# Where a norm and its first panel stand in a decoder step: the program's head as one stage by thirds of the tokens, and the second mixer's norm inside the first MLP's last part

## The chip, the cores and the metric

The kernel runs on one core of one Trainium2 chip. The metric is the device time of one execution in microseconds (us); lower is better. A core has five engines that run their own instruction streams and meet through semaphores: TensorE (PE in the profile, with its weight loads as PEld), VectorE (DVE), ScalarE (ACT), GpSimd (POOL) and SyncE (SP), which here only issues DMAs.

## The reference

One step of a decoder with two layers over 1,056 tokens: 1,024 of a prompt and 8 sequences of 4 sample tokens. Width 1,024, float32 throughout.

```
for l in range(DEPTH):                     # DEPTH = 2
    if l < N_SELF:                         # layer 0: mLSTM matrix memory ("first mixer")
        mix, (c, n, m) = mlstm_layer(rmsnorm(h, norm_mix[l]), ..., w_in_a[l], ..., w_out_a[l])
    else:                                  # layer 1: stick-breaking attention ("second mixer")
        kv = rmsnorm(h, norm_kv) @ w_kv
        q = (rmsnorm(h, norm_mix[l]) @ w_q_b[j])
        o = stick_breaking_attention(q, k_all, v_all, sb_bias[j], past_len)
        mix = o @ w_out_b[j]
    h = h + mix
    u = rmsnorm(h, norm_mlp[l]) @ w_up[l]
    h = h + jnp.square(jax.nn.relu(u)) @ w_down[l]
y = rmsnorm(h, norm_final)
```

`rmsnorm(x, g)` is `x * rsqrt(mean(x*x) + 1e-6) * g`, over the features of a token.

## The kernel before

**Layout.** The residual `h` stays in SBUF with features on partitions: `m.h` is [128, 8, 1056], 8 feature tiles (`KT`) of 128. Tokens are cut into three thirds (`NT = 3`) of 352 (`TW`). Each float32 product is made of three matmuls: x is split into `x_hi` (rounded) and `x_lo` (the rest), each weight panel of 128 output features into `w_hi` and `w_lo`, and hi*hi, lo*hi and hi*lo are added in PSUM. One output tile (128 features by a third of the tokens) is 24 matmuls of 128x352, a panel is three tiles, 72 matmuls.

**Weights.** There are two weight slots. SP loads a panel into `w_raw[slot]`, POOL splits it (`split_panel`: a multiply by the norm's gain where there is one, a CAST to `w_hi`, a TENSOR_TENSOR to `w_lo`), and PE uses it. The first two panels of a mixer or MLP are loaded and split at the end of the part before (`head_loads`, `head_splits`; class `Head` holds their semaphores).

**Norm.** `rms` is not applied before the product: panels are multiplied with the raw split of h, and `rms_inverse` scales the result when it is read from PSUM. So a norm is: on ACT `x_hi` (8 ACTIVATEs) and squares (8), on DVE `x_lo` (8) and the sum of the squares (`norm_add`, 8), on PE one matmul per third with a matrix of ones (`norm_pe`), on ACT a Ln per third and one Exp (`norm_act_rs`). `dense_first` runs the first panel feature tile by feature tile while `x_lo` is being made: the 9 matmuls of tile k wait for x count k+1.

**Order.** The program is a chain of phases, each an `nc.Block`: all engines finish one before any begins the next.

1. `constants`: POOL fills masks and the identity; SP loads five gains and the page table.
2. `embed`: SP loads nine row blocks of x, PE transposes them (4 transposes to a bank, 4 banks), DVE and ACT copy the banks to `h` by turns; POOL splits the first two panels.
3. `mixer_a`: on ACT and DVE the norm of all tokens, on PE the gate panel (`w_in_a`'s last 128 columns), then the norm's sums; POOL meanwhile makes fills (`filled`, 12 of them) and then splits. DVE scales the gate rows into `graw`, PE picks the 16 gate rows out (L830), and DVE runs a long chain over 8 rows from L1052 on, while PE runs the first four panels. Each panel tile goes to one of two banks and waits for the bank's read-out by DVE, which stands inside that chain. ACT spills `h` to HBM (`h_spill`), for the residual.
4. `out_and_mlp`: output projection, then 8 chunks of 4 up panels and 4 down double-panels. Down tiles are added to `h` by DVE. The chunks are a hardware loop.
5. `mixer_b`: semaphores are cleared and the engines meet once more, then SP loads the biases, two panels, spills `h`, and loads pages of the cache; ACT, DVE and PE do the norm and the first panel (q). Then come the k panel (3 tiles), page transposes, the v panel, and the attention.
6. `out_and_mlp` again, and `final`.

Of the kernel before, what the change touches and what calls it, by code (L numbers as in the profile page):

```python
# [106 lines left out]
def weight_turns(eng, stages, panel):  # L107

    n = tiles = before = 0
    for turns, panels in stages:  # L110
        per, per_tiles = len(panels), sum(x[1] for x in panels)
        assert per % 2 == 0
# [65 lines left out]
class Head:  # L178
# [3 lines left out]
    def __init__(self, own, panels):  # L182
        self.w, self.panels = weight_sems(own.sem), panels


def head_loads(sp, m, head, w=None, panels=0):

    for slot, (ap, _) in enumerate(head.panels):
        if w is not None:

            sp.wait_ge(w.split, panels - 1 + slot)
        load_panel(sp, m, head.w, slot, ap)
# [36 lines left out]
def dense_first(pe, m, w, n, slot, before, x, between=None):  # L229
# [6 lines left out]
    for k in range(KT):  # L236
        if k == KT // 2 and between is not None:
            between()
        pe.wait_ge(x, k + 1)
        for t in range(NT):  # L240
            wh, wl = m.whi[slot][:, k * P:(k + 1) * P], m.wlo[slot][:, k * P:(k + 1) * P]
            xh, xl = m.xhi[:, k, t * TW:(t + 1) * TW], m.xlo[:, k, t * TW:(t + 1) * TW]
            pe.matmul(m.bank[t][:, 0:TW], wh, xh, start=(k == 0), stop=False)
            pe.matmul(m.bank[t][:, 0:TW], wh, xl, start=False, stop=False)
            last = pe.matmul(m.bank[t][:, 0:TW], wl, xh, start=False, stop=(k == KT - 1))
            if k == KT - 1:
                last.then_inc(w.tile_ready, 1)
# [57 lines left out]
def norm_pe(pe, m, s):  # L305

    pe.wait_ge(s.acc, KT)
    for t in range(NT):
        pe.matmul(m.bank[3 + t][:, 0:TW], m.ones[:, :], m.acc[:, t * TW:(t + 1) * TW], start=True, stop=True)\
# [3 lines left out]
def norm_act_rs(act, m, s):  # L313

    for t in range(NT):
        act.wait_ge(s.sum, t + 1)
        act.activation(m.rs[:, t * TW:(t + 1) * TW], m.bank[3 + t][:, 0:TW], ACT.Ln, bias=m.eps[:, 0:1],
# [6 lines left out]
def constants(nc, m, own):  # L324

    made, landed = own.sem("constants_made"), own.sem("gains_landed")
    with nc.Block() as block:
        @block.gpsimd
        def _(pool):
            pool.memset(m.ident[:, :], 0.0).then_inc(made, 1)  # L330
            pool.memset(m.identb[:, :], 0.0).then_inc(made, 1)
            pool.memset(m.ones[:, :], 1.0).then_inc(made, 1)
# [5 lines left out]
            pool.memset(m.eps[:, :], EPS).then_inc(made, 1)  # L338
            pool.wait_ge(made, 9)
            n = 9  # L340
# [8 lines left out]
            keep(m.ident[:, :], ALU.not_equal, 1.0, 0, [[-1, P]], 1)  # L349
# [8 lines left out]

            for j in range(SG):
# [4 lines left out]

        @block.sync
        def _(sp):
            gains = [(m.g_mix[l], m.d["norm_mix"][l]) for l in range(2)]
            gains += [(m.g_mlp[l], m.d["norm_mlp"][l]) for l in range(2)]
            gains += [(m.g_kv, m.d["norm_kv"])]
            with nc.allow_non_contiguous_dma(reason="five gains of 4 KB, a feature to a partition"):  # L370
                for tile, src in gains:
                    sp.dma_start(tile[:, :], src.rearrange("(k p) -> p k", p=P)).then_inc(landed, 16)
            sp.dma_start(m.ptab[:, :], m.d["page_table"].rearrange("b (o g) -> o (b g)", o=1)).then_inc(landed, 16)
            sp.wait_ge(landed, 16 * len(gains) + 16)

def embed(nc, m, own):

    with ExitStack() as c:  # L380
        xin = own.tensor("x_rows", [P, NB, D], F32)
        landed = [own.sem(f"x_landed{b}") for b in range(NB)]
        turned, free_dve, free_act = own.sem("x_turned"), own.sem("x_bank_free_dve"), own.sem("x_bank_free_act")
        block = c.enter_context(nc.Block())

        @block.sync
        def _(sp):
            for b in range(NB):
                t0, n = blocks_of(b)
                src = m.d["x_prompt"][0, t0:t0 + n, :] if b < NC else m.d["x_sample"].rearrange("b t d -> (b t) d")  # L390
                sp.dma_start(xin[0:n, b, :], src).then_inc(landed[b], 16)
            head_loads(sp, m, m.heads[0])

        @block.gpsimd
        def _(pool):
            head_splits(pool, m, m.heads[0])

        @block.tensor
        def _(pe):
            g = 0  # L400
            for b in range(NB):
                n = blocks_of(b)[1]
                pe.wait_ge(landed[b], 16)
                for half in range(2):
                    if g >= 4:

                        pe.wait_ge(free_act if g % 2 else free_dve, (g - 4) // 2 + 1)
                    for q in range(4):
                        k = 4 * half + q
                        last = pe.transpose(m.bank[g % 4][:, q * P:q * P + n], xin[0:n, b, k * P:(k + 1) * P],  # L410
                                            m.ident[0:n, 0:n])
                    last.then_inc(turned, 1)
                    g += 1

        def read_out(eng, op, which, free):
            for g in range(which, 2 * NB, 2):
                t0, n = blocks_of(g // 2)
                eng.wait_ge(turned, g + 1)
                src = m.bank[g % 4][:, :].rearrange("p (q t) -> p q t", q=4)[:, :, 0:n]
                op(m.h[:, 4 * (g % 2):4 * (g % 2) + 4, t0:t0 + n], src).then_inc(free, 1)  # L420

        @block.vector
        def _(dve):
            read_out(dve, dve.tensor_copy, 0, free_dve)

        @block.scalar
        def _(act):
            read_out(act, act.copy, 1, free_act)
# [87 lines left out]
def mixer_a(nc, m, own):  # L516
# [66 lines left out]
    with ExitStack() as c:  # L583
# [25 lines left out]
        w, s = m.heads[0].w, norm_sems(own.sem)  # L609
        filled, landed = own.sem("fills"), own.sem("a_landed")  # L610
        spilled, gathered = own.sem("h_spilled"), own.sem("pages_gathered")
# [20 lines left out]
        panels = [(lambda i: last128, NT), (lambda i: last128, 0)] + [panel_in(*x) for x in PANELS]  # L632
# [34 lines left out]
        def _(pool):  # L667
# [22 lines left out]
            head_splits(pool, m, m.heads[1], w, (TILES - NT, TILES))  # L690

        @block.tensor
        def _(pe):
            def third(tau, part):

                n = (tau - TAU0) // NT + 2
                t = tau % NT
                bank = m.bank[tau % 2]
                if part == 0:
                    pe.wait_ge(w.split, n + 1)  # L700

                    pe.wait_ge(w.tile_free[0], tau - 1)
# [129 lines left out]
            for tau in range(TAU0, TAU0 + FIRST_TILES):  # L832
# [33 lines left out]
        def _(act):  # L866
            norm_act(act, m, s, m.h, m.g_mix[0])
            for kk in range(KT):
                act.dma_start(m.spill[kk], m.h[:, kk, :]).then_inc(spilled, 16)
            norm_act_rs(act, m, s)  # L870
# [140 lines left out]
        def _(dve):  # L1011
            norm_dve(dve, m, s, m.h, m.g_mix[0])
# [29 lines left out]
            for t in range(NT):  # L1042
# [3 lines left out]
                dve.tensor_tensor(graw[:, ts], m.bank[t][:, 0:TW], m.rs[:, ts], ALU.mult).then_inc(w.tile_free[0], 1)  # L1046
# [172 lines left out]
def mixer_b(nc, m, own):  # L1219
# [61 lines left out]
    with ExitStack() as c:  # L1281
# [17 lines left out]
        w, s = m.heads[2].w, norm_sems(own.sem)  # L1299
        landed, spilled, filled, chain = own.sem("b_landed"), own.sem("h_spilled"), own.sem("fills"), own.sem("dve_step")  # L1300
# [60 lines left out]
        def _(eng):  # L1361
# [15 lines left out]
            for kk in range(KT):  # L1377
# [729 lines left out]
```

## Time and profile before

| | |
|---|---|
| median of 3 runs | 3087.38 us (3086.38 to 3090.63) |
| profiled execution | 3094.23 us |
| its span, first to last instruction | 3092.4 us |
| PE busy | 2893.2 us, 94% |
| DVE / ACT / POOL busy | 45% / 26% / 24% |
| granted TensorE clock, mean | 0.974 |

A row of the timeline gives start and duration of a group of like instructions on one engine, its line, what it writes and reads, and in brackets how long the engine stood idle before it and what ended the wait. The times below are of the profiled execution and count from its first instruction.

### The profile page before, as it was taken

The numbers are of one execution on the slowest core, as the hardware profiler recorded it, in microseconds if no ns is written. First come the engines' busy times: TensorE is split into PE (matmuls) and PEld (weight loads), VectorE is DVE, ScalarE is ACT, GpSimd is POOL, SyncE is SP. The second block draws the span as 40 slices with busy tenths as digits, with TensorE's granted clock in tenths as the row PEclk, the third lists the DMA queues.
The fourth block names the chain that finished last, engine by engine and source line by source line (L and its number), as shares of the span: only waits on it lengthen the run. The fifth ranks groups of instructions, "written<-read, shape, count | busy, mean of one in ns | idle before, by whom it ended". The sixth has DMA issues, their size and how long they took to land. (4 is left out here: it accounts for less than half of the span.)

```text
span 3092.4 us, 49344 instructions
## 1 busy us (share of the span) xinstructions
PE 2893.2 (94%) x19749; PEld 2634.2 (85%) x19749; DVE 1378.7 (45%) x1993; ACT 818.4 (26%) x1647; POOL 756.2 (24%) x452
## 2 busy tenths in 40 slices
PE   5999997999999999978999899898799999999998
PEld 4989887999999999976766677666599999999997
DVE  4422334444433344444546554655545433344434
ACT  3120222211110011124555545555512110011112
POOL 4212111322323323332111211120122332332331
PEclk8999998999999999989999999999899999999999
DMA  5666444233233232223333433343411111111112
GB/s 160 177 149 193 83 29 92 73 92 96 81 95 95 81 95 87 89 97 96 107 109 98 121 97 114 100 119 91 147 48 42 48 42 47 47 41 47 47 41 77
DMA packets 362482, 277.68 MB, mean 90 GB/s; under 512 B 31394, under 2 KB 353954, under 8 KB 360290
## 3 DMA queue, kind: packets, MB, share of 16 engines
q1 hardware_dynamic: 341002, 258.18, 28.8%
q10 hardware_dynamic: 21336, 17.47, 2.9%
q8 instruction: 104, 1.70, 0.2%
q14 instruction: 40, 0.33, 0.0%
HBM read 251.58 MB, written 91.11 MB: 111 GB/s over the span
## 5 line engine op out<-in xcount | busy, mean ns | idle before, releaser
L162 POOL CAST w_hi<-w_raw 128x1024 fp32r<-128x1024 f32 x194 | 208.6, 1075 | 1661.1 <-PE bank L214 902.0
L212 PE MATMUL bank<-p_u_hi,w_hi 128*128 128x352 f32 x1536 | 496.5, 323 | 14.5 <-DVE p_u_lo L2001 14.5
L212 PE MATMUL bank<-x_hi,w_hi 128*128 128x352 f32 x1536 | 496.9, 323 | 2.9 <-DVE p_q L1758 2.9
L213 PE MATMUL bank<-p_u_lo,w_hi 128*128 128x352 f32 x1536 | 495.5, 323 | 0.0
L214 PE MATMUL bank<-p_u_hi,w_lo 128*128 128x352 f32 x1536 | 495.3, 322 | 0.0
L214 PE MATMUL bank<-x_hi,w_lo 128*128 128x352 f32 x1536 | 494.5, 322 | 0.0
L213 PE MATMUL bank<-x_lo,w_hi 128*128 128x352 f32 x1536 | 494.0, 322 | 0.0
L164 POOL TENSOR_TENSOR w_lo<-w_raw,w_hi 128x1024 fp32r<-128x1024 f32 x194 | 483.8, 2494 | 15.6
L2009 DVE TENSOR_TENSOR h<-bank,h 128x352 f32<-128x352 f32 x384 | 199.9, 524 | 492.5 <-PE bank L214 492.5
L1961 ACT ACTIVATE p_relu<-bank 128x352 f32<-128x352 f32 x192 | 89.1, 464 | 1039.5 <-PE bank L214 1033.2
L212 PEld LDWEIGHTS bank<-p_u_hi,w_hi 128*128 128x128 f32 x1536 | 288.5, 188 | 18.7 <-issue 18.7
L212 PEld LDWEIGHTS bank<-x_hi,w_hi 128*128 128x128 f32 x1536 | 289.1, 188 | 4.7 <-issue 4.7
L213 PEld LDWEIGHTS bank<-x_lo,w_hi 128*128 128x128 f32 x1536 | 290.0, 189 | 0.0
L214 PEld LDWEIGHTS bank<-x_hi,w_lo 128*128 128x128 f32 x1536 | 289.3, 188 | 0.0
L214 PEld LDWEIGHTS bank<-p_u_hi,w_lo 128*128 128x128 f32 x1536 | 288.6, 188 | 0.0
L213 PEld LDWEIGHTS bank<-p_u_lo,w_hi 128*128 128x128 f32 x1536 | 288.6, 188 | 0.0
L1785 DVE TENSOR_TENSOR_SCAN square<-square,zero 128x512 f32<-128x512 f32 (+5 forms) x192 | 212.7, 1131 | 124.1 <-ACT square L1643 122.3
L1997 DVE TENSOR_TENSOR p_relu<-p_relu,rms_inverse 128x352 f32<-128x352 f32 x192 | 133.4, 695 | 275.5 <-ACT p_relu L1961 275.5
L1999 DVE CAST p_u_hi<-p_relu_sq 128x352 fp32r<-128x352 f32 x192 | 162.9, 849 | 108.5 <-ACT p_relu_sq L1963 108.5
L706 PE MATMUL bank<-x_hi,w_hi 128*128 128x352 f32 x576 | 200.0, 347 | 0.0
L708 PE MATMUL bank<-x_hi,w_lo 128*128 128x352 f32 x576 | 186.2, 323 | 0.0
L707 PE MATMUL bank<-x_lo,w_hi 128*128 128x352 f32 x576 | 185.8, 323 | 0.0
(247 smaller groups left out, 4587.7 us busy)
## 6 DMA issues: line engine op xcount, KB each, us to landing
k_pages<-in_cache_k SPq DMA_DIRECT2D x64, 512.0 KB, 5.7
w_raw<-in_w_up SPq DMA_DIRECT2D x64, 512.0 KB, 4.0
v_pages<-in_cache_v SPq DMA_DIRECT2D x64, 512.0 KB, 4.8
w_raw<-in_w_down SPq DMA_DIRECT2D x64, 512.0 KB, 3.4
p_pages<-k_pages SPq DMA_DIRECT2D x256, 128.0 KB, 2.4
p_pages<-v_pages SPq DMA_DIRECT2D x256, 128.0 KB, 2.3
w_raw<-in_w_in_a SPq DMA_DIRECT2D x26, 512.0 KB, 4.5
h<-h_spill ACTq DMA_DIRECT2D x16, 528.0 KB, 8.6
```

Source lines behind the costliest of these rows:

```text
L162: pool.tensor_copy(m.whi[slot][:, :], m.wraw[slot][:, :]).then_inc(w.hi, 1)
L164: pool.tensor_tensor(m.wlo[slot][:, :], m.wraw[slot][:, :], f32(m.whi[slot][:, :]), ALU.subtract)\
L212: pe.matmul(bank[:, 0:TW], wh, xh, start=(k == 0), stop=False)
L213: pe.matmul(bank[:, 0:TW], wh, xl, start=False, stop=False)
L214: last = pe.matmul(bank[:, 0:TW], wl, xh, start=False, stop=(k == nk - 1))
L706: pe.matmul(bank[:, 0:TW], wh, xh, start=(kk == 0), stop=False)
L707: pe.matmul(bank[:, 0:TW], wh, xl, start=False, stop=False)
L708: last = pe.matmul(bank[:, 0:TW], wl, xh, start=False, stop=(kk == KT - 1))
L1785: dve.tensor_tensor_scan(stick, stick, m.zero[:, 0:1].broadcast_to([P, hi - lo]), sticks[h2][:, hi:hi + 1] if x else 1.0, ALU.mult, ALU.ad ...
L1997: dve.tensor_tensor(relu[t][:, :], relu[t][:, :], m.rs[:, toks], ALU.mult).then_inc(scaled, 1)
L1999: dve.tensor_copy(uhi[:, u, toks], sqr[t][:, :]).then_inc(hi_ready, 1)
L2009: dve.tensor_tensor(ht, m.bank[t][:, 0:TW], ht, ALU.add).then_inc(w.tile_free[t], 1)
```

## The change

**Head.** `constants` and `embed` become one phase, `start`, that also holds the first norm. SP loads x first (three blocks, then the gate panel, then the rest), and the gains last; ACT's queue loads the one gain that the first norm needs. Work goes by thirds of the tokens (row blocks 0 to 2, 3 to 5, 6 to 8): copies to `h`, `x_hi` and `x_lo` of that third, then the gate panel's tile of that third on PE. Squares of a third are one ACTIVATE of 128x2816, and are added pairwise by DVE (1408, 704, 352 columns). PE sums a third at a time. ACT copies two banks of three, DVE one. `h` is spilled from SP's queue. POOL splits the gate panel and, in the other slot, the first real panel. `mixer_a` then starts with that panel's first tile, the fills and `graw`.

**Boundary.** The first `out_and_mlp` gets `norm_after = 1`: its eighth chunk is taken out of the loop. After the three adds of feature tile k, ACT makes `x_hi` and the square of it, DVE `x_lo` and the sum; SP spills it. After the last down tile PE runs the q panel (`dense_first`, now to banks 5 to 7) with the norm's sums ahead of its feature tile 6. `mixer_b` loses all of this and starts with the k panel. The negated biases move behind the fifth read-out.

```diff
-def dense_first(pe, m, w, n, slot, before, x, between=None):
+def dense_first(pe, m, w, n, slot, before, x, between=None, at=KT // 2, bank0=0):
...
+        @block.tensor                       # start()
...
+            for g in range(2 * TO[1]):
+                turn(g)
+            gates(0)
+            for g in range(2 * TO[1], 2 * NB):
+                turn(g)
+            gates(1)
+            pe.wait_ge(made, 2)
+            wait_taken(pe, 2 * NB)
+            sums(0)
+            gates(2)
+            sums(1)
+            sums(2)
...
+        @block.scalar
...
+            copies(0)
+            high(0)
+            copies(1)
+            high(1)
+            square(0)
+            copies(2)
+            high(2)
+            square(1)
+            square(2)
+            act.wait_ge(made, 2)
+            norm_act_rs(act, m, s, 2)
...
-            dense_first(pe, m, w, 0, 0, 0, s.x)     # mixer_a, PE
-            norm_pe(pe, m, s)
+            for part in range(len(THIRDS)):
+                third(TAU0, part)
             pe.wait_ge(w.tile_free[0], NT)
             pe.wait_ge(filled, 12)
-            pe.wait_ge(s.rs, 1)
...
@@ mixer_b, SP
             for n in range(2, 4):
                 weights(n)
-            for kk in range(KT):
-                eng.dma_start(m.spill[kk], m.h[:, kk, :]).then_inc(spilled, 16)
@@ mixer_b, PE, ACT, DVE
-            dense_first(pe, m, w, 0, 0, 0, s.x)
-            norm_pe(pe, m, s)
-            norm_act(act, m, s, m.h, None)
-            norm_act_rs(act, m, s)
-            norm_dve(dve, m, s, m.h, None)
@@ out_and_mlp, SP
+                for k in range(KT):
+                    for t in range(NT):
+                        sp.wait_ge(w.tile_free[t], USES_OUT + (CH - 1) * USES_C + UT + k + 1)
+                    sp.dma_start(m.spill[k], m.h[:, k, :]).then_inc(after.spilled, 16)
@@ out_and_mlp, PE
+            if norm_after:
+                turn(CH - 1, 0)
+                def sums():
+                    pe.wait_ge(w.tile_free[2], USES_OUT + CH * USES_C)
+                    norm_pe(pe, m, after.s, 2)
+                dense_first(pe, m, after.w, 0, 0, 0, after.s.x, between=sums, at=KT - 2, bank0=5)
@@ out_and_mlp, ACT
+                turn(CH - 1)
+                for k in range(KT):
+                    for t in range(NT):
+                        act.wait_ge(w.tile_free[t], USES_OUT + (CH - 1) * USES_C + UT + k + 1)
+                    act.activation(m.xhi[:, k, :], m.h[:, k, :], ACT.Copy).then_inc(after.s.hi, 1)
+                    norm_square(act, m, after.s, m.h, k)
+                norm_act_rs(act, m, after.s, 2)
@@ out_and_mlp, DVE
+                    if ending:
+                        dve.wait_ge(after.s.hi, k + 1)
+                        dve.tensor_tensor(m.xlo[:, k, :], m.h[:, k, :], f32(m.xhi[:, k, :]), ALU.subtract).then_inc(after.s.x, 1)
+                        norm_add(dve, m, after.s, k)
```

Two places show what moves. DVE at the head of the program before, from its first instruction to the start of the gate chain:

```order
L420 COPY h<-bank 128x4x128 x8
L420 COPY h<-bank 128x4x32
L284 SCALAR_TENSOR_TENSOR x_lo<-h,g_mix,x_hi 128x1056 x8
L292 COPY squares<-square 128x1056
L295 TENSOR_TENSOR squares<-squares,square 128x1056 x7
L1046 TENSOR_TENSOR square<-bank,rms_inverse 128x352 x3
L1052 TENSOR_SCALAR p_numerator<-bank,p_gate_bias 8x352
```

and of the change, up to the last `x_lo`; the three adds of lines 515 to 519 then follow twice more:

```order
L462 COPY h<-bank 128x4x128 x2
L509 SCALAR_TENSOR_TENSOR x_lo<-h,g_mix,x_hi 128x352 x8
L462 COPY h<-bank 128x4x128 x2
L509 SCALAR_TENSOR_TENSOR x_lo<-h,g_mix,x_hi 128x352 x8
L462 COPY h<-bank 128x4x128 x2
L515 TENSOR_TENSOR p_x_rows<-p_x_rows 128x1408
L517 TENSOR_TENSOR p_x_rows<-p_x_rows 128x704
L519 TENSOR_TENSOR squares<-p_x_rows 128x352
L509 SCALAR_TENSOR_TENSOR x_lo<-h,g_mix,x_hi 128x352 x8
```

The norm's work is now between the copies, in pieces of a third, and only the last third's stands behind the last copy.

DVE around the boundary of the first MLP and the second mixer before (the last add of the loop, then the mixer):

```order
L2009 TENSOR_TENSOR h<-bank,h 128x352
L284 SCALAR_TENSOR_TENSOR x_lo<-h,x_hi 128x1056 x8
L292 COPY squares<-square 128x1056
L295 TENSOR_TENSOR squares<-squares,square 128x1056 x7
L1747 TENSOR_SCALAR p_minus_bias<-p_bias 128x16
L1748 TENSOR_SCALAR p_minus_bias_sample<-p_bias_sample 128x8
L1758 SCALAR_TENSOR_TENSOR p_q<-bank,rms_inverse 128x352 x3
```

and of the change, feature tiles 0, 1 and 7 of the last chunk and what follows:

```order
L2126 TENSOR_TENSOR h<-bank,h 128x352 x3
L2129 TENSOR_TENSOR x_lo<-h,x_hi 128x1056
L292 COPY squares<-square 128x1056
L2126 TENSOR_TENSOR h<-bank,h 128x352 x3
L2129 TENSOR_TENSOR x_lo<-h,x_hi 128x1056
L295 TENSOR_TENSOR squares<-squares,square 128x1056
...
L2126 TENSOR_TENSOR h<-bank,h 128x352 x3
L2129 TENSOR_TENSOR x_lo<-h,x_hi 128x1056
L295 TENSOR_TENSOR squares<-squares,square 128x1056
L1849 SCALAR_TENSOR_TENSOR p_q<-bank,rms_inverse 128x352 x3
```

Two instructions over 1,056 columns now stand between the adds that free PE's banks; the mixer starts with the read-out of q.

## Rows read from the trace of the kernel before

**Rows 1.** The page: busy time, PE's busy tenths in 40 slices.

```profile
PE 2893.2 (94%) x19749; PEld 2634.2 (85%) x19749; DVE 1378.7 (45%) x1993; ACT 818.4 (26%) x1647; POOL 756.2 (24%) x452
PE   5999997999999999978999899898799999999998
```

**Rows 2.** Timeline of PE, 0 to 70 us.

```profile
14.08 6.24 PE L410 MATMUL bank<-identity,p_x_rows 128*128 128x128 f32 x40 [14.08 <-DMA p_x_rows<-in_x_prompt]
57.99 3.76 PE L309 MATMUL bank<-squares,ones 128*128 128x352 f32 x6 [8.11 <-DVE squares L295]
65.22 3.56 PE L830 MATMUL bank<-square,p_pick_gates 128*128 128x352 f32 x6 [3.47 <-DVE square L1046]
68.35 0.59 PE L706 MATMUL bank<-x_hi,w_hi 128*128 128x352 f32 x1
```

**Rows 3.** Timelines of ACT, DVE, SP and POOL, 2 to 90 us.

```profile
2.27 1.09 SPq L372 DMA_DIRECT2D g_mix<-in_norm_mix  x2
10.27 3.87 SPq L391 DMA_DIRECT2D p_x_rows<-in_x_prompt  x8
16.08 0.58 ACT L420 COPY h<-bank 128x512 f32<-128x512 f32 x1 [14.07 <-PE bank L410]
33.02 0.20 POOL L668 MEMSET p_pick_gates<- 128x128 f32 x1 [0.31 <-POOLq L380]
41.59 2.04 ACT L270 ACTIVATE square<-h 128x1056 f32<-128x1056 f32 x2
40.59 1.58 POOL L686 COPY p_pair_rows<-identity 8x512 f32<-8x512 f32 x1
61.19 1.44 ACT L317 ACTIVATE rms_inverse<-bank,eps 128x352 f32<-128x352 f32 x3 [7.46 <-PE bank L309]
63.77 1.39 DVE L1046 TENSOR_TENSOR square<-bank,rms_inverse 128x352 f32<-128x352 f32 x3 [5.84 <-ACT rms_inverse L320]
68.93 0.57 DVE L1052 TENSOR_SCALAR p_numerator<-bank,p_gate_bias 8x352 f32<-8x352 f32 x1 [3.77 <-PE bank L830]
86.66 0.50 DVE L1038 TENSOR_TENSOR p_v_next<-bank,rms_inverse 128x352 f32<-128x352 f32 x1
```

**Rows 4.** Timeline of PE, 1340 to 1402 us.

```profile
1346.00 0.32 PE L214 MATMUL bank<-p_u_hi,w_lo 128*128 128x352 f32 x1
1383.33 0.63 PE L212 MATMUL bank<-x_hi,w_hi 128*128 128x352 f32 x1 [2.90 <-DVE p_q L1758]
1400.76 1.07 PE L1536 MATMUL bank<-p_page_keys_t,p_q_sample 128*32 128x512 f32 x8 [0.68 <-ACT p_page_keys_t L1684]
```

**Rows 5.** Timelines of DVE, POOL and SP, 1346 to 1383 us.

```profile
1346.50 1.90 POOL L158 TENSOR_TENSOR w_raw<-w_raw,g_kv 128x1024 f32<-128x1024 f32 x1 [5.95 <-issue]
1349.68 2.34 POOL L164 TENSOR_TENSOR w_lo<-w_raw,w_hi 128x1024 fp32r<-128x1024 f32 x1
1353.60 0.32 POOL L1420 MEMSET p_q_sample<- 128x256 f32 x1 [1.59 <-POOLq L2085]
1364.91 11.59 DVE L295 TENSOR_TENSOR squares<-squares,square 128x1056 f32<-128x1056 f32 x7
1370.67 2.70 POOL L158 TENSOR_TENSOR w_raw<-w_raw,g_kv 128x1024 f32<-128x1024 f32 x1 [16.75 <-PE bank L245]
1355.50 0.62 SPq L1372 DMA_DIRECT2D w_raw<-in_w_kv  x1
```

**Rows 6.** Writers of w_raw, 1353 to 1400 us: its last line.

```profile
DMA to landing us min/median/max: 13.3/13.7/14.1
```

**Rows 7.** Windows: busy time of PE, PEld, DVE, ACT, POOL; PEclk, DMA share, GB/s.

```profile
1383.00:1389.00 6.00, 5.67 (x19) 5.70 (x20) 0.97 (x4) 0.00 (x0) 0.00 (x0) 0.50 0.02 5
1353.60:1364.00 10.40, 7.86 (x33) 7.89 (x34) 9.26 (x8) 9.86 (x10) 0.32 (x1) 0.60 0.04 1
```

**Rows 8.** Timeline of PE in the first MLP's own norm.

```profile
604.69 1.94 PE L309 MATMUL bank<-squares,ones 128*128 128x352 f32 x6
606.19 0.59 PE L243 MATMUL bank<-x_hi,w_hi 128*128 128x352 f32 x1
```

More of the change, by code:

```diff
@@ L236, in dense_first @@
     for k in range(KT):
-        if k == KT // 2 and between is not None:
+        if k == at and between is not None:
             between()
@@ L378, in embed @@
[L378 to L396, printed above, removed]
+            split(1)
@@ new lines, in sums @@
+            def sums(t):
+                pe.wait_ge(s.acc, t + 1)
+                pe.matmul(m.bank[2 + t][:, 0:TW], m.ones[:, :], m.acc[:, t * TW:(t + 1) * TW], start=True, stop=True)\
+                    .then_inc(s.sum, 1)
+            for g in range(2 * TO[1]):
[7 more added lines that the diff above has]
+            sums(0)
@@ new lines, in _, with take, copies, high @@
+            gates(2)
+            sums(1)
+            sums(2)
+        def take(eng, op, free, g):
+            t0, n = blocks_of(g // 2)
+            eng.wait_ge(turned, g + 1)
+            src = m.bank[g % 4][:, :].rearrange("p (q t) -> p q t", q=4)[:, :, 0:n]
+            op(m.h[:, 4 * (g % 2):4 * (g % 2) + 4, t0:t0 + n], src).then_inc(free, 1)
+        @block.scalar
+        def _(act):
+            with nc.allow_non_contiguous_dma(reason="a gain of 4 KB, a feature to a partition"):
+                act.dma_start(m.g_mix[0][:, :], m.d["norm_mix"][0].rearrange("(k p) -> p k", p=P)).then_inc(gain_in, 16)
+            def copies(t):
+                for g in range(2 * TO[t - 1] if t else 0, 2 * TO[t]):
+                    if g % AT_DVE:
+                        take(act, act.copy, free_act, g)
+            def high(t):
+                ts = slice(t * TW, (t + 1) * TW)
+                wait_taken(act, 2 * TO[t])
+                if t == 0:
+                    act.wait_ge(gain_in, 16)
+                for k in range(KT):
+                    act.activation(m.xhi[:, k, ts], m.h[:, k, ts], ACT.Copy, scale=m.g_mix[0][:, k:k + 1]).then_inc(s.hi, 1)
+            def square(t):
+                ts = slice(t * TW, (t + 1) * TW)
+                act.activation(squares[t].rearrange("p (k t) -> p k t", k=KT), m.h[:, :, ts], ACT.Square).then_inc(s.sq, 1)
+            copies(0)
[9 more added lines that the diff above has]
+            norm_act_rs(act, m, s, 2)
@@ L422, in _, with copies, low @@
         @block.vector
         def _(dve):
[L424 to L428, printed above, removed]
+            def copies(t):
+                for g in range(2 * TO[t - 1] if t else 0, 2 * TO[t]):
+                    if g % AT_DVE == 0:
+                        take(dve, dve.tensor_copy, free_dve, g)
+            def low(t):
+                ts = slice(t * TW, (t + 1) * TW)
+                for k in range(KT):
+                    dve.wait_ge(s.hi, t * KT + k + 1)
+                    dve.scalar_tensor_tensor(out=m.xlo[:, k, ts], in0=m.h[:, k, ts], scalar=m.g_mix[0][:, k:k + 1],
+                                             in1=f32(m.xhi[:, k, ts]), op0=ALU.mult, op1=ALU.subtract).then_inc(s.x, 1)
@@ L1832, in _, with out_and_mlp @@
                         sample_queries(pq)
-def out_and_mlp(nc, m, own, w_out, w_up, w_down, gain, gather, head, after):
+def out_and_mlp(nc, m, own, w_out, w_up, w_down, gain, gather, head, after, norm_after):
     with ExitStack() as c:
```

229 lines of the change are left out of this document (143 added, 86 removed).

## The prediction

> **What bounds the kernel now.** I read the page first: PE is busy 94% of the span, and its tenths are below 8 in two places that the change touches, the first slice and the eighteenth [rows 1]. So what the change can give is PE's idle and half-speed time there. Then I read PE's timeline in both places, row by row, for what ended each idle stretch. At the head PE waits for the first rows of x until 14.08, for the sum of the squares until 57.99 and for the gate rows until 65.22; DVE starts its chain over the gate rows at 68.93 [rows 2, 3]. At the boundary the last down tile ends at 1346.3, and the k panel, the first that needs the norm to be over, starts at 1383.33 [rows 4]. The reader should see that in both places the chain runs over ACT and DVE: one norm over 1,056 tokens, with PE beside it and then behind it.
>
> **The head, step by step.** What PE does later hangs on the start D of DVE's chain, 68.93 now: read-outs of PE's two banks stand inside it, and PE's first tiles cannot run ahead. The read-out at 86.66 is the sharpest case: PE's sixth tile needs that bank, free at 87.2, and comes to it at 68.35 + 5 x 3.84 = 87.5 now [rows 2]. In the change the first tile is done before the pick, so PE comes one tile (3.84 us, 24 matmuls at 0.16) earlier to that bank and is held there. The tile done early is therefore worth 0.3 us, and the gain is the shift of D.
>
> D after, from the program's start: x is issued where the gains are now, at 2.27 instead of 10.27 [rows 3], so PE has the first rows at 6.1 instead of 14.1. The copies of the first third need about 5 us more: 11. From there ACT is the longest chain. A piece of 352 columns takes it 1.44/3 = 0.48, a square of 1,056 columns 1.02 [rows 3], so 2,816 columns about 2.6. Three times 8 pieces 11.5, three squares 7.8, the copies left 4.5 (8 at 0.58), 1 of waits: 36. DVE then adds the last third's squares: 2,464 columns at the 1.66 us per 1,056 of the adds now (11.59/7) [rows 5] would be 3.9, undisturbed less, I take 3: 39. Sum, Ln and Exp took 57.99 to 63.77 for three thirds [rows 2, 3]; two of the three are done earlier: 3.5. So the mixer's phase starts at S = 43, with ends 42 and 46 (PE at half speed in the two gate tiles that ACT's copies wait for).
>
> What is late next is POOL. The pick needs the 12 fills, and they run from 33.02 to 42.17 [rows 3], 9.2 us, now hidden beside x_lo and the gate panel. In the change their cover is one tile of PE and graw (1.39). They may be shorter without DVE's big operations beside them; no row shows how much. I bound them by 9.2 and by 6.5, which has the copy (1.58 for 8 rows) and the two selects before it at a third, and take 8. The pick and its wait take 68.93 - 65.22 = 3.7 at half speed, about 2 at full speed; after a tile of matmuls I take 3. D = 43 + 8 + 3 = 54, and **the head gives 15 us**; ends: 42 + 6.5 + 2 = 50.5 gives 18, 46 + 9.2 + 3.7 = 58.9 gives 10. The first weight split after the fills is not late: PE has two tiles of the panel before it left, 7.7 us, for 3.4 us of POOL.
>
> **The boundary.** In the last chunk DVE gets two operations per feature tile. Undisturbed, from the last down tile of k: add 0.5, ACT's x_hi 1.1 and its latency 0.3, x_lo 1.25, the sum 1.35, next add 0.5: 5.0 us, and PE needs that bank back after three tiles, 5.8 us. So nothing is late in even k. In odd k POOL splits a panel at the same moment. DVE's seven adds took 11.59; POOL's split began at 1370.67, so about four lie before it, 1.4 each, and three share the 5.8 us behind it, 1.9 to 2.0 each [rows 5]. Then x_lo and sum are 4.0 instead of 2.6, and PE stalls 0.6 to 1 in k = 1, 3 and 5. I take 2.5 in all, with ends 0 and 4. The upper end is a wait for whole operations: x_lo is due 2 us after the tile, POOL's w_lo (2.34) runs from 1.3 to 3.7 behind it, and where the gain's multiply (1.90) comes first, w_lo meets the sum instead [rows 5]; 1.2, 1.2 and 1.8 us make 4.2. The Trainium skill (page "SBUF — State Buffer", section "SBUF: two separate sides") has that as the rule: DVE with two SBUF inputs and GpSimd exclude each other for a whole instruction. By that rule the term is 4.2 instead of 2.5.
>
> Then PE: q panel 72 x 0.16 = 11.5, the sums 606.19 - 604.69 = 1.5 [rows 8] and 0.3 of tail, behind which ACT's Ln and Exp are hidden; end of the phase and cleared semaphores 1.6 (POOL's 1353.60) [rows 5]. The mixer starts at 1346.3 + 2.5 + 11.5 + 1.5 + 0.3 + 1.6 = 1363.7, and PE with the k panel there instead of at 1383.33: 19.6 us.
>
> Not all of it lasts. The v panel starts at 1401.8 now, when the page transposes end [rows 4]. It needs w_raw of v, which SP issues behind the biases: 1.9 us after the mixer's start, and it lands 13.3 to 14.1 later [rows 5, 6], since nothing moves until 1364 (DMA share 0.04, 1 GB/s) [rows 7]. Now the norm hides that. In the change it is 15.2 after the start, POOL's split with gain is 5.5 (1346.50 to 1352.02) [rows 5]: v can start 20.7 after the mixer does. PE alone would be there after 1401.8 - 1383.3 = 18.5, less 3 at full speed, 15.5; so it waits, first for pages, which SP issues behind that panel, and then for the split. v starts at 1363.7 + 20.7 = 1384.4, 17.4 us earlier. After idle of 2.90 us PE ran at clock 0.50 for 6 us [rows 4, 7], which costs half of it; the k panel has that now too, the v panel does not, and after a wait of 3 to 5 us it would: I take 1.5 off. **The boundary gives 16 us**; ends: 11 (all stalls, v panel at half speed for long), 23 (v's panel lands early, full speed: 19.6 and the 3 us that half speed costs now). The spill moves to SP's idle queue in the MLP and costs nothing; uncovered it would be 3.4 us, DVE's wait before the first read-out of q now. Unrolling a chunk and one phase fewer I put at nothing.
>
> **Sum.** 15 + 16 = 31 us: 3094.2 to 3063 in the profiled execution. That one is 6.8 us above the median of the three runs; I take the difference over: 3087.4 - 31 = **3056**. A measurement of this kernel tells about 0.2%, 6 us, from no change.
>
> **The rivals.**
> *The boundary gives everything* (chance 0.12). For it: 8 us of the empty DMA time lie in the biases' small reads, and if v's panel gets in front of them, PE goes through. Against it: the landings of 13.3. Gain 15 + 23 = 38, with a good head 41: 3046 to 3050.
> *The head gives little* (0.16). If PE is at half speed through gate panel and pick, S is 46 or later and DVE's adds are slowed by the split of the second panel. Gain 5 to 10 there, 16 at the boundary: about 3064.
> *The last chunk is paced by DVE and POOL* (0.09): operations wait for each other whole. For it: a 2.3 us operation of POOL meets DVE's in each odd tile; against it: DVE's adds beside POOL went on at 2.0 each [rows 5]. The stalls are 4.2, or up to 8 where even tiles inherit the delay, x_lo and the sum of the last tile come late too, and v's split meets the k read-outs: gain 15 + 8 = 23, 3064. It is the rule of the page named above.
> *No change* (0.03): both PE waits come back in full, the gate chain behind the fills and the k panel behind the pages; needs 31 us of new waits, of which I find 9.
> *Slower* (0.03), one mechanism: in the last chunk each feature tile holds its bank until DVE has done x_lo and sum. Above 5.8 us per tile that delay is PE's. It decides from 31/8 = 3.9 us beyond that, 9.7 per tile; I find 5.0 to 6.9. At 11 us per tile it would be 3087 + 11 = 3098.
>
> **Chances.** Forecast (gain 25 to 37, 3050 to 3062) 0.57, the rivals as given. Faster 0.94, same 0.03, slower 0.03. The range holds the forecast and most of the three gaining rivals: 3046 to 3067.
>
> **What would show it.** Right: DVE's first TENSOR_SCALAR of the gate chain at 54, behind PE's pick, which POOL's copy of pair rows releases; the mixer's phase starting at 43; PE's first matmul of the k panel at about 1363.7 less the head's 15, with an idle of under 2 us before it; and a wait of 3 us or more ahead of the v panel, for POOL's split. Wrong: PE idle over 1 us between down tiles of the last chunk; the fills done before PE's first tile ends; page transposes at once behind the k panel.

## The result, and the profile after

The changed kernel takes 3059.85 us (median of 4 runs, 3056.07 to 3063.72), the kernel before 3088.77 beside it: ratio 0.9907, 95% interval 0.9889 to 0.9925. That is 28.9 us. The two profiled spans are 3061.9 and 3092.4 us, 30.5 apart. The forecast was 3056 with a gain of 31, its range 3046 to 3067.

The page after, with PE's tenths and the granted clock. The first slice has gone from 5 to 7, the eighteenth from 7 to 8 [rows 1].

```profile
span 3061.9 us, 49302 instructions
PE 2885.6 (94%) x19749; PEld 2625.2 (86%) x19749; DVE 1377.0 (45%) x2007; ACT 821.6 (27%) x1661; POOL 751.6 (25%) x450
PE   7999997999999999988898899888799999999998
```

**The head.** Timelines of PE, POOL and DVE of the changed kernel, which answer to [rows 2, 3].

```profile
20.11 1.94 PE L425 MATMUL bank<-identity,p_x_rows 128*128 128x128 f32 x8 [4.54 <-DVE h L462]
46.56 0.63 PE L812 MATMUL bank<-x_hi,w_hi 128*128 128x352 f32 x1 [2.01 <-PEq L328]
52.93 2.01 PE L935 MATMUL bank<-square,p_pick_gates 128*128 128x352 f32 x6 [0.42 <-POOL p_pair_rows L791]
...
46.52 0.20 POOL L773 MEMSET p_pick_gates<- 128x128 f32 x1 [21.39 <-POOLq L328]
51.78 0.19 POOL L785 TENSOR_SCALAR_AFFINE_SELECT p_pick_gates<-p_pick_gates 128x8 f32<-128x8 f32 x1
52.18 0.60 POOL L791 COPY p_pair_rows<-identity 8x512 f32<-8x512 f32 x1
...
13.92 5.44 DVE L509 SCALAR_TENSOR_TENSOR x_lo<-h,g_mix,x_hi 128x352 fp32r<-128x352 f32 x8 [2.42 <-ACT x_hi L480]
55.09 0.57 DVE L1152 TENSOR_SCALAR p_numerator<-bank,p_gate_bias 8x352 f32<-8x352 f32 x1 [7.08 <-PE bank L935]
72.50 0.50 DVE L1138 TENSOR_TENSOR p_v_next<-bank,rms_inverse 128x352 f32<-128x352 f32 x1
```

Read it from the end: DVE's chain over the gate rows starts at 55.09 instead of 68.93, behind PE's pick; the pick waited 0.42 us for POOL's copy of the pair rows, the last of the fills, which run from 46.52 to 52.78. The read-out that stood at 86.66 [rows 3] stands at 72.50: the head gave 14.2 us.

**The boundary.** Timelines of PE, SP, POOL and DVE where the second mixer starts; [rows 4, 5] have the same places before.

```profile
1347.56 0.40 PE L212 MATMUL bank<-x_hi,w_hi 128*128 128x352 f32 x1 [1.66 <-PEq L2210]
1369.18 1.07 PE L1635 MATMUL bank<-p_page_keys_t,p_q_sample 128*32 128x512 f32 x8 [0.68 <-ACT p_page_keys_t L1777]
...
1347.89 1.46 SPq L1467 DMA_DIRECT2D p_bias_sample<-in_sb_bias  x2
1349.40 0.62 SPq L1473 DMA_DIRECT2D w_raw<-in_w_kv  x1
1356.94 13.05 SPq L1490 DMA_DIRECT2D p_pages<-k_pages  x16
...
1362.75 1.89 POOL L158 TENSOR_TENSOR w_raw<-w_raw,g_kv 128x1024 f32<-128x1024 f32 x1 [14.91 <-DMA w_raw<-in_w_kv]
1365.92 2.35 POOL L164 TENSOR_TENSOR w_lo<-w_raw,w_hi 128x1024 fp32r<-128x1024 f32 x1
```

The k panel starts at 1347.56, 35.8 us earlier than in [rows 4]; the products with the page keys, behind which the v panel starts, at 1369.18 instead of 1400.76, 31.6 us earlier. Less the head's 14.2 the boundary gave 21.6 and then 17.4; of the two spans' difference of 30.5 it has 16.3. What held PE between the two stands in the list of PE's waits from 1280 to 1500 us (total, times, longest):

```profile
PE bank L1585 <- DMA p_pages<-k_pages: 5.5, 1, 5.5
PE bank L212 <- DVE h L2126: 1.4, 2, 0.7
```

The wait of 5.5 is for the key pages. POOL's split of v ends at 1368.3 (1365.92 + 2.35), two microseconds before PE starts the v panel (its first matmul stands at 1370.18).

### The profile page after: what moved, and what is told of

It is laid out like the page before. It is cut to its first block and busy times, and to the rows that moved or that the text cites. A ratio compares the mean times of both kernels' runs of the same rounds, so it can differ in the third digit from the quotient of the medians.

```text
span 3061.9 us, 49302 instructions
## 1 busy us (share of the span) xinstructions
PE 2885.6 (94%) x19749; PEld 2625.2 (86%) x19749; DVE 1377.0 (45%) x2007; ACT 821.6 (27%) x1661; POOL 751.6 (25%) x450
## 5 line engine op out<-in xcount | busy, mean ns | idle before, releaser
L164 POOL TENSOR_TENSOR w_lo<-w_raw,w_hi 128x1024 fp32r<-128x1024 f32 x193 | 480.8, 2491 | 15.5
```

What stands on the lines that cost most here:

```text
L164: pool.tensor_tensor(m.wlo[slot][:, :], m.wraw[slot][:, :], f32(m.whi[slot][:, :]), ALU.subtract)\
```

## The experiments

Each is the changed kernel with one edit, unless it says otherwise; "before" is the run of that kernel beside it.

### The halves apart

```diff
 head only:      new start and mixer_a; out_and_mlp and mixer_b as before
 boundary only:  constants, embed, mixer_a as before; out_and_mlp and mixer_b of the change
```

> The new start phase and its first mixer, with the MLP and the second mixer as before. If the two halves of the gain are independent and the head's share is the shift of DVE's gate chain (68.93 before, 55.09 after), this run is 14 us faster than before (13 to 15), and DVE's gate chain starts at 55. If the profiled 14 at the head were partly given back later in the first mixer, it is 10 or less faster; if the head carries more than the profile shows, 18 or more.

> The constants, embed and first mixer as before, with the norm in the MLP's last chunk. If the boundary's share is the rest of what the trace shows (v panel 31.6 us earlier, 14.4 of them from the head), this run is 15 to 17 us faster than before, with 1.4 us of PE stalls in the last chunk and a wait of about 5.5 us for the key pages ahead of the v panel. Rival: the two halves share something (the k_pages gather, the queue), and then the sum of this run and the head-only run misses the 29 us of the change by more than 4.

Head only: 3071.39 us (before 3086.78), ratio 0.9951 [0.9934, 0.9967], 15.4 us. Boundary only: 3071.24, ratio 0.9947 [0.9934, 0.9961], 15.5 us. In the second, PE stalls 1.4 us in the last chunk and waits 5.46 us for the pages. The sum, 30.9, is the change's 28.9 within what such medians tell (the runs of the head alone go from 3064.5 to 3079.6): nothing that the halves share shows.

### The queue behind the boundary: biases and pages

```diff
 mixer_b, SP (biases behind weights)
-    bias, sbias: three small loads      # 8 KB, and twice 2 KB of every second bias
     weights(2); weights(3)              # w_raw of v and q
+    bias, sbias: three small loads
     load_page(0..15)
 biases early: the same three loads stand in out_and_mlp's SP, behind head_loads
 of the last chunk; their two tiles are allocated ahead of the phases' own
```

> The change, with the three bias loads behind the two weight loads and ahead of the pages. Theory A, the biases hold up what is issued behind them: v's weights land about 4 us after issue, POOL's split begins before 1354 instead of 1362.75, but the pages are still behind the biases, so the wait ahead of the page transposes stays at 4 to 7 us and the time is that of the change within 2 us. Theory B, the v panel hangs on POOL's split: the v panel starts 5 us earlier and the kernel is 4 to 5 us faster than the change.

> The change, with the three small bias loads taken out of the second mixer's queue and issued in the MLP's last chunk. Theory A, the biases' small reads hold up the queue: v's weights land about 3 to 5 us after their issue instead of 13.2, POOL's split of v begins before 1353 instead of at 1362.75, PE goes from the k panel to the page transposes without a wait, and the v panel starts at about 1364.7 instead of 1370.25: 5 us faster than the change (4 to 6), 34 faster than before. Theory B, the first reads of the phase are late for another reason (w_raw or the queue itself): v's weights still land 10 us or more after their issue and the time is that of the change within 1 us. Theory C, the pages come in time and the wait moves on to the q panel's split: 1 to 3 us faster.

Behind the weights: 3061.32 us (before 3088.92), ratio 0.992 [0.9905, 0.9936], no gain over the change, as theory A has it (its four runs lie between 3052.1 and 3067.7, so the time alone says little). Timelines of POOL, SP and PE of that run:

```profile
1353.25 1.90 POOL L158 TENSOR_TENSOR w_raw<-w_raw,g_kv 128x1024 f32<-128x1024 f32 x1 [5.59 <-DMA w_raw<-in_w_kv]
...
1352.67 16.50 SPq L1489 DMA_DIRECT2D p_pages<-k_pages  x16
...
1364.06 3.86 PE L1584 MATMUL bank<-identity,p_pages 128*128 128x128 f32 x16 [4.99 <-DMA p_pages<-k_pages]
```

The split of v begins 5.9 us after the phase's start instead of 15.2, and PE still waits 4.99 us for a page: the split was not what the v panel hung on. The list of loads of that run shows what the pages stand behind (KB each, median us to landing):

```profile
w_raw<-in_w_kv SPq DMA_DIRECT2D x1, 512.0 KB, 5.7
p_bias_sample<-in_sb_bias SPq DMA_DIRECT2D x2, 2.0 KB, 9.8
```

and in the change, where they stand first:

```profile
p_bias_sample<-in_sb_bias SPq DMA_DIRECT2D x2, 2.0 KB, 10.0
```

Two kilobytes take longer than 512, in either place. The Trainium skill (page "DMA: Bandwidth & Descriptors", section "Rules for kernel authors") says that a strided last dimension becomes one descriptor for each element; these loads are of that kind (every second bias, 4 bytes), and the count of packets agrees: 1,488 under 512 bytes from 1346 to 1375 us of the change, 340 from 1340 to 1375 in the run below, which has these loads elsewhere. Two loads of 512 elements are 1,024 of the difference. That the number of packets is what makes them slow is not shown.

Early: 3042.78 us (before 3086.78), ratio 0.9857 [0.9841, 0.9873]. POOL, PE and DVE of that run:

```profile
1343.58 0.32 POOL L1514 MEMSET p_q_sample<- 128x256 f32 x1 [7.43 <-POOLq L2211]
1349.36 1.90 POOL L158 TENSOR_TENSOR w_raw<-w_raw,g_kv 128x1024 f32<-128x1024 f32 x1 [5.46 <-DMA w_raw<-in_w_kv]
...
1355.29 1.03 PE L1580 MATMUL bank<-identity,p_pages 128*128 128x128 f32 x8
1363.50 0.52 DVE L1850 TENSOR_TENSOR p_v_next<-bank,rms_inverse 128x352 f32<-128x352 f32 x1 [7.49 <-PE bank L215]
```

PE's page transposes come without a wait for a page, and the first v read-out stands 19.9 us after the phase's start instead of 26.8: 7 us, a little over the 4 to 6 expected. But the kernel gained 17 by the medians, and the phase itself starts 4 us earlier than in the change. Some ten microseconds came from somewhere else.

### Where the other ten came from: an address

```diff
     m.g_kv = sb("g_kv", [P, KT])
+    sb("unused", [P, 8])        # 32 bytes; [P, 24], 96 bytes, in the other run
```

> The change, with 32 bytes of unused SBUF ahead of each phase's own tiles and nothing else. The run with the biases early was 17 us faster than the change where the trace had 7 us for it behind the mixer's start; in its MLPs PE went through 3730 matmuls in 600 us instead of 3712, though no instruction there differs. Its two bias tiles moved u_hi and u_lo from an address that leaves 32 over 64 (and over 128) to one that leaves nothing. Theory A, a matmul reads its rows faster from an address that is a multiple of 64: this shift makes it one (it leaves 64 over 128), so 3728 to 3732 matmuls in the two windows of 600 us, and 7 to 10 us faster than the change. Theory B, it has to be a multiple of 128, or the address plays no part: 3712, and within 3 us of the change.

> The change, with 96 bytes of unused SBUF ahead of each phase's own tiles, the same shift as the two bias tiles made. Theory A, the address of u_hi and u_lo is what made the MLPs faster: 3728 to 3732 matmuls in each window of 600 us, 7 to 10 us faster than the change, with the wait of 5.5 us for the pages still there. Theory B, it was something else in the run with early biases: 3712, within 3 us of the change.

> The biases early, with 32 bytes more of unused SBUF, so that u_hi and u_lo lie as in the change (32 over a multiple of 64). Theory A, of the 17 us the queue's order gives 5.5 to 7 and the address the rest: 3712 matmuls in the windows of 600 us, v read-out 19.9 us after the mixer's start as before, and 5 to 8 us faster than the change. Theory B, all 17 us come from the biases' move: 14 us or more faster than the change.

The windows 650 to 1250 and 2350 to 2950 us lie in the two MLPs (busy time and, in brackets, instructions of PE, PEld, DVE, ACT, POOL; PEclk, DMA share, GB/s). Of the change:

```profile
650.00:1250.00 600.00, 594.52 (x3712) 592.96 (x3711) 234.50 (x382) 71.76 (x149) 180.07 (x103) 1.00 0.30 91
```

With 32 bytes:

```profile
650.00:1250.00 600.00, 594.55 (x3716) 592.99 (x3714) 234.97 (x382) 71.96 (x150) 180.62 (x104) 1.00 0.31 90
```

With 96 bytes:

```profile
650.00:1250.00 600.00, 594.42 (x3731) 592.88 (x3730) 237.43 (x386) 73.28 (x152) 182.53 (x104) 1.00 0.30 89
```

With the biases early, without and with 32 bytes more:

```profile
650.00:1250.00 600.00, 594.44 (x3730) 592.90 (x3729) 237.81 (x385) 72.77 (x151) 182.57 (x104) 1.00 0.30 90
```

```profile
650.00:1250.00 600.00, 594.55 (x3713) 592.98 (x3712) 234.47 (x382) 71.25 (x148) 178.90 (x102) 1.00 0.31 91
```

All at full clock; the second window gives the same counts within one. By the order and sizes of the kernel's tiles `u_hi` starts at byte 146,464 of a partition in the change, which leaves 32 over 128; shifted by 32 it leaves 64, by 96 nothing; with the biases early nothing, and 32 with the extra bytes. (No profile shows addresses.) The count goes with that remainder: 3712 and 3713 where it is 32, 3715 and 3716 where it is 64, 3730 and 3731 where it is nothing, in these runs and in the others. One thing has to be counted beside it: once in each chunk's down tiles PE waits 0.9 us for DVE's `u_lo`, and a window holds six or seven of these waits. With seven the count is 3706, as in the kernel before and in the second window of the run with the stores moved back, at the same remainder of 32.

Is it the rows that a matmul reads, then? A chunk's up panels read `x_hi` and `x_lo`, which are allocated ahead of the added bytes and do not move; its down tiles read `u_hi` and `u_lo`, which do. Timeline of PE over one chunk of the change (first up matmul, first down matmul, first up matmul of the next chunk):

```profile
677.80 0.32 PE L212 MATMUL bank<-x_hi,w_hi 128*128 128x352 f32 x1
723.75 0.32 PE L212 MATMUL bank<-p_u_hi,w_hi 128*128 128x352 f32 x1
771.00 0.32 PE L212 MATMUL bank<-x_hi,w_hi 128*128 128x352 f32 x1
```

and with 96 bytes:

```profile
676.10 0.32 PE L212 MATMUL bank<-x_hi,w_hi 128*128 128x352 f32 x1
721.88 0.32 PE L212 MATMUL bank<-p_u_hi,w_hi 128*128 128x352 f32 x1
768.86 0.32 PE L212 MATMUL bank<-x_hi,w_hi 128*128 128x352 f32 x1
```

The down tiles take 46.98 us instead of 47.25, but the up panels take 45.78 instead of 45.95, though nothing that they read has moved. Every full chunk of both MLPs shows the same, within some hundredths of a microsecond. So the shift of the tiles is shown to be the cause, and what it acts through is not: two fifths of the effect lie where the rows read stand still. What does move there is what ACT and DVE write meanwhile (`relu`, `relu_sq`, `u_hi`, `u_lo`). The 0.44 us of a chunk make 7 us in the 16 chunks of the two MLPs.

Times: 32 bytes 3065.3 us, ratio 0.9919 [0.9903, 0.9935], 5.4 above the change's median; 96 bytes 3050.85, ratio 0.9879 [0.9858, 0.99], 9.0 us below the change's median, though the two intervals overlap; biases early with 32 bytes 3054.64, ratio 0.989 [0.9871, 0.9909], 5.2 below. Of the expectations, theory A held for 96 bytes and for the biases early with 32. For 32 bytes alone neither held as written: a multiple of 64 is not enough (3716 where A had 3728 or more), and B's "within 3 us" was missed too. Of the 17 us, 5 to 7 are the queue's order and 9 to 12 the shift by the medians (9.0 against the change, 11.9 with the biases early in both), 7 of them seen in the MLPs' chunks.

### The residual stores back in the mixer's queue

```diff
 out_and_mlp, SP
-    for k: wait for the k-th feature tile of h; spill[k] <- h[k]
 mixer_b, SP
     weights(2); weights(3)
+    for kk: spill[kk] <- h[kk]
     load_page(0..15)
```

> The change, with the eight stores of h back in the second mixer's queue, behind the two weight loads and ahead of the pages, as before. Theory A, the pages are what the v panel waits for: eight stores of 528 KB ahead of them (8.18 us of issue in the start phase) move the first page and the v panel 8 to 12 us later, and DVE's first read-out of q waits for the stores too, about 15 us: 8 to 16 us slower than the change. Theory B, as the forecast had it, moving the stores costs or gives at most the 3.4 us of DVE's wait before: 0 to 4 us slower than the change.

3075.70 us (before 3088.92), ratio 0.9964 [0.9951, 0.9977]: 15.9 us slower than the change. SP, DVE and PE of that run:

```profile
1355.87 11.30 SPq L1479 DMA_DIRECT2D h_spill<-h  x8
...
1373.51 1.39 DVE L1851 SCALAR_TENSOR_TENSOR p_q<-bank,rms_inverse 128x352 f32<-128x352 f32 x3 [36.79 <-DMA h_spill<-h]
...
1376.10 0.63 PE L212 MATMUL bank<-x_hi,w_hi 128*128 128x352 f32 x1 [21.69 <-DVE p_k L1857]
```

The stores go behind the biases too. DVE's first read-out of q waits for them until 1373.5, and PE stands 21.69 us in the k panel for a bank. The norm in the MLP alone, without this move, would have given nothing that these runs can show: this one is no faster than the head alone (3071.39). Theory A held, at its upper end.

### The start phase: DVE's copies between its x_lo pieces

```diff
-    low(0); copies(1); wait_taken(..); low(1); copies(2)
+    low(0, (6, 9)); wait_taken(..); low(1, (12, 15))   # a copy ahead of pieces 3 and 6
```

> The change, with DVE's copies of the second and third third of x put between its x_lo pieces instead of behind them. Theory A, the start phase is 3.5 us longer than forecast because PE's transposes wait for DVE's copies, which stand behind 5.4 us of x_lo (PE waited 4.54 us for one, and ACT 3.15 us for PE): ACT's wait at 18 to 21 goes, the mixer's phase starts at about 43.5 instead of 46.5, and the kernel is 2 to 3 us faster than the change. Theory B, ACT's own work is what sets the phase: start at 46 or later, within 1 us of the change.

3056.86 us (before 3088.92), ratio 0.9897 [0.9883, 0.9911], 3.0 below the change's median, within its interval. PE of that run:

```profile
17.02 1.06 PE L425 MATMUL bank<-identity,p_x_rows 128*128 128x128 f32 x8 [0.46 <-DVE h L462]
44.42 0.63 PE L812 MATMUL bank<-x_hi,w_hi 128*128 128x352 f32 x1 [2.01 <-PEq L328]
```

The wait of 4.54 us for a copy is 0.46, and the mixer's phase starts 2.1 us earlier. That is theory A, though not its whole size: ACT ends its last square 4.0 us earlier (35.68 instead of 39.63), but DVE ends its last add only 2.5 earlier. The saving in time alone is not settled.

### The pick ahead of the first tile

```diff
 mixer_a, POOL
+    pick: memset, two selects; then the other fills
 mixer_a, PE
-    third(TAU0, 0..2); pe.wait_ge(filled, 12); pick
+    pe.wait_ge(filled, 3); pick; third(TAU0, 0..2)
 mixer_a, DVE
-    dve.wait_ge(filled, 12)                      # ahead of the gate chain
+    dve.wait_ge(filled, 4); ...; dve.wait_ge(filled, 12)   # the rest behind two read-outs
```

> The change, with the pick matrix filled first on POOL and PE's pick ahead of its first tile. If DVE's gate chain is what the head's gain hangs on, and PE's tile done early is worth 0.3 us, DVE's chain starts at about 50.5 instead of 55.09 and the kernel is 4 to 5 us faster than the change, 33 to 34 faster than before. Rival: once the chain starts early, PE's first tiles (at half speed until 50.7) or the split of the second panel (w_raw lands at 54.37) are what comes last, and 2 us or less is left.

3060.11 us (before 3086.78), ratio 0.9915 [0.9901, 0.993]: the change's time, so the rival, but by other waits than it named. DVE and POOL:

```profile
52.67 0.57 DVE L1149 TENSOR_SCALAR p_numerator<-bank,p_gate_bias 8x352 f32<-8x352 f32 x1 [4.48 <-DMA p_g_head<-in_head_norm_a]
56.26 2.35 DVE L1153 TENSOR_SCALAR p_states<-square 8x1056 f32<-8x1056 f32 x1
71.71 0.50 DVE L1135 TENSOR_TENSOR p_v_next<-bank,rms_inverse 128x352 f32<-128x352 f32 x1
...
55.66 2.39 POOL L164 TENSOR_TENSOR w_lo<-w_raw,w_hi 128x1024 fp32r<-128x1024 f32 x1
```

The chain waits until 52.67 for the head gains, a small load that SP issues when the phase starts. It then meets POOL's w_lo: an operation of 0.70 us in the change takes 2.35 here and ends 0.6 us after POOL's. Of 2.4 us at the start 0.8 are left at the read-out (71.71 against 72.50).

### POOL's w_lo twice in the last chunk

```diff
 split_panel, first panel of the second mixer
+    wlo <- wraw - whi           # once more, the same result
     wlo <- wraw - whi
```

> The change, with POOL's w_lo of the q panel computed twice in the last chunk (2.4 us more of POOL, the same result). By the theory that DVE waits for POOL's whole operation (x_lo 3.02 us beside w_lo 2.41, 1.26 alone): the second w_lo starts at about 1328.3, x_lo of the seventh feature tile, due at 1328.54, lasts 3.3 to 3.5 instead of 1.26, and PE waits 1.0 to 1.3 us more for a bank. By the theory that the two only slow each other down: x_lo 1.9 to 2.1 and no further wait of PE.

One run, 3059.13 us. POOL and DVE:

```profile
1328.45 2.41 POOL L167 TENSOR_TENSOR w_lo<-w_raw,w_hi 128x1024 fp32r<-128x1024 f32 x1
...
1328.64 3.33 DVE L2133 TENSOR_TENSOR x_lo<-h,x_hi 128x1056 fp32r<-128x1056 f32 x1 [1.24 <-ACT x_hi L2084]
```

x_lo took 3.33 us as the theory of whole operations has it (3.3 to 3.5), against 1.26 for the same tile in the change. The second half of that expectation missed: PE waited no longer (1.4 us in all, as in the change). The tile held was the seventh; only the eighth comes after it in those banks, and then the q panel, which has banks of its own.

### All three edits

> The change with the three edits together: the biases early (with the address that comes with it), the pick ahead of the first tile, and DVE's copies between its x_lo pieces. One by one they gave 17, 0 to 1 and 3 us by the medians, with DVE's gate chain 2.4 us earlier by the pick first (then held by a small load of the head gains, landed at 52.6) and 1.9 by the copies. If they add up: gate chain at 50.5 to 51, 19 to 21 us faster than the change, about 3040 us. If the chain's start no longer decides what follows (as the run with the pick first says, 2.4 us earlier there and 0 to 2 in the end): 17 to 19 us faster.

3039.17 us (before 3088.69), ratio 0.9838 [0.982, 0.9856]: 49.5 us below before and 20.7 below the change. DVE's chain starts at 50.71. The gain is what adding up forecast (19 to 21 us, the chain at 50.5 to 51). It is the fastest kernel of this study, and 17.1 of the 20.7 come with the biases' move and the shift that it brought (3042.78 alone). The 3.6 us between those two runs' medians are within their intervals (0.9841 to 0.9873 and 0.982 to 0.9856).

## Why the prediction was right, step by step

**The head, 15 forecast; 14.2 in the trace, 15.4 by itself.** Three terms were off and nearly cancelled, which is luck. The mixer's phase starts at 46.5, not 43. Of these 3.5 us, 2.2 lie in the first third, where ACT comes to x_hi at 13.19 instead of 11. The rest is a wait that I had at 1 us: ACT stood 3.15 us for PE, which stood 4.54 us for a copy that DVE had behind 5.44 us of x_lo; the run with the copies between starts the phase 2.1 earlier. The fills took 6.3 us, not 8: where DVE's large operations stood beside them before, a select took 1.0 to 1.3 us, and now 0.19. The pick with what follows up to DVE took 2.3 instead of 3. So D is 46.5 + 6.3 + 2.3 = 55.1, against 54.

**The end of the chain, right.** The gate chain hangs on the pick and the pick on POOL's pair rows, as forecast. That an earlier start D moves everything behind it one for one is true for the change; the run with the pick first shows its limit, 2.4 us at D and 0.8 at the read-out.

**The last chunk, 2.5 forecast, 1.4 measured.** PE stalls twice by 0.7. The mechanism was the upper end's: timelines of DVE and POOL of the changed kernel,

```profile
1297.60 3.02 DVE L2129 TENSOR_TENSOR x_lo<-h,x_hi 128x1056 fp32r<-128x1056 f32 x1 [1.24 <-ACT x_hi L2080]
1304.31 1.26 DVE L2129 TENSOR_TENSOR x_lo<-h,x_hi 128x1056 fp32r<-128x1056 f32 x1 [1.24 <-ACT x_hi L2080]
...
1297.09 2.41 POOL L164 TENSOR_TENSOR w_lo<-w_raw,w_hi 128x1024 fp32r<-128x1024 f32 x1
```

x_lo beside w_lo lasts until 1.1 us after POOL's end, 3.02 instead of 1.26, and the longer split above stretched it to 3.33. By the Trainium skill's rule (page "SBUF — State Buffer", section "SBUF: two separate sides") the two exclude each other for a whole instruction; the trace agrees. But my 4.2 us for that rule counted each hold as PE's; 1.8 us of hold cost 0.7 of stall, since the banks had about 1 us in hand, and in the third case, where the gain's multiply came first, both were held a little: DVE's sum took 2.08 instead of 1.25, POOL's cast 1.84 instead of 1.04 and its w_lo 3.29 instead of 2.4, with no stall of PE. My own 2.5 came from operations that slow each other down in part, with three stalls of 0.6 to 1; x_lo was held whole instead, and there were two stalls.

**The boundary, 16 forecast; 17.4 at the v panel, 15.5 by itself.** The k panel came 21.6 us earlier (forecast 19.6; 1.1 of the 2.0 are stalls that did not come). The v panel came 17.4 earlier, as forecast before the 1.5 that I took off for a slow clock; the v panel did not get that (its first read-out stands 4.1 us behind its start). The equal 17.4 is luck: v starts 22.7 us after the mixer does, not 20.7, and this ate up the 2.0 that the k panel had gained. The size was right and the cause half wrong. I had v wait "first for pages, and then for the split"; the split was ready 2 us before v started, the wait of 5.5 us was for pages alone, and the run with the biases behind the weights shows that an early split gives nothing. So the last of my signs of being right, a wait for POOL's split, missed. What comes late is one thing, the biases' small reads, and the pages stand behind them in either order.

**The step that failed: "costs nothing; uncovered it would be 3.4 us".** Moving the stores was free, but their cover had gone with the norm, and left in the old place they cost 15.9 us, not 3.4. The 3.4 was not even theirs. The stores, ACT and DVE of the kernel before:

```profile
L1378 SPq DMA_DIRECT2D h_spill<-h x8: 434/1126/3995, 1363.2 to 1373.5; - x8
DMA to landing us min/median/max: 5.2/6.4/7.9
...
1381.06 1.08 ACT L320 ACTIVATE rms_inverse<-rms_inverse 128x1056 f32<-128x1056 f32 x1
...
1382.23 1.39 DVE L1758 SCALAR_TENSOR_TENSOR p_q<-bank,rms_inverse 128x352 f32<-128x352 f32 x3 [3.42 <-issue]
```

The last store, issued at 1373.5, landed at 1380.8 by the trace; the Exp that makes `rms_inverse` ended at 1382.14, and DVE's read-out of q, which needs both, came right behind the Exp. So there the stores cost nothing, and a wait that ended with something else told nothing of their length. What tells it is the time from the phase's start to the last landing: 27.2 us before (1353.6 to 1380.8), hidden by a norm of 28.6, and 27.0 with the stores moved back, with nothing in front. The move is worth the whole of the boundary's gain.

**The rivals.** "The boundary gives everything" did not occur in the change, but its mechanism is real: with the biases out of the way PE does not wait for pages, for 5 to 7 us, where that rival had 7. The head gave its share, the last chunk was not paced by DVE, and the two rivals without a gain found no place.

## What to carry to other kernels

When a long operation ahead of a queue is taken away, look up everything that was hidden behind it and cost it from the phase's start to its landing, not by a wait that was left: here stores of 4 MB stood beside 3.4 us of wait and cost 15.9 once bare. A few hundred strided 4-byte elements were a 10 us load here; issue them a phase early. And if a kernel speeds up where nothing was edited, compare instruction counts in a fixed window at full clock (and how many of a loop's stalls fall into it), then the addresses.

## What the runs showed of the hardware that I had not expected

**PE's pace by the place of a phase's tiles.** With `u_hi` and `u_lo` at a multiple of 128 bytes PE gets through 3731 matmuls of 352 columns in 600 us, 32 bytes beside it through 3712: 0.5%, 7 us in the MLPs' chunks and some 9 us of this kernel by the medians. 64 over a multiple of 128 gave 3716. Matmuls that read unmoved tiles gained too (45.95 to 45.78 us for a chunk's up panels), so it is not, or not only, the address of the rows that a matmul reads. That DVE's or ACT's accesses play a part is not excluded; PE had no waits of theirs that differed. No run moves one of these tiles alone.

**DVE held with one input.** In the run with the pick first, DVE's multiplication of one SBUF tile (8 rows, 1,056 columns) was held by POOL's w_lo, 2.35 us instead of 0.70, and 2.32 in the run with all three edits; both times it ended 0.6 us after POOL's operation. Two SBUF inputs are not needed for it.

**Open.** Runs of one kernel differ by up to 16 us (3052.1 to 3067.7 with the biases behind the weights), and the second mixer's middle differs between profiles by 12 (from v's first read-out to the second MLP's last split of h, 823.9 us in the change's profile and 811.8 with the biases behind the weights), with waits for value pages and dips of the clock in other places each time. What sets these was not tried.
